# Final-state store no longer waited for at startup, one GLU block under the first norm, fourteen key copies on ScalarE

## What is computed

```python
q, k, v, u = project(x, w_in)                  # 1024 -> 4*512
a = diff_attention(q, k, v, ...)               # 4 heads
s, h_re, h_im = s5_mixer(u, ...)               # SSM scan; h_re, h_im: final states, outputs
#   inside: y = gelu(y); out = y * sigmoid(y @ w_glu + b_glu)        (the GLU)
x1 = layer_norm(ALPHA * x + concat(a, s) @ w_out, ln1_g, ln1_b)
# PEER: per token and each of 8 heads
q = rms_norm(x1 @ w_q); s = q . sub_keys; top 16 of each half, top 16 of 256 sums -> 128 experts in all
act = gelu(u_tab[idx] . x1);  out = sum(g * act * v_tab[idx])
y = layer_norm(ALPHA * x1 + out, ln2_g, ln2_b)
```

## Time and profile before

| what | value |
|---|---|
| three timed runs | 3626.15, 3635.01, 3638.67 us; median 3635.01 |
| profiled execution, time | 3620.71 us |
| its span, first to last instruction | 3618.9 us |
| busy share: PE, DVE, ACT, POOL | 71%, 67%, 42%, 35% |
| mean granted TensorE clock | 0.799 of full |
| DMA mean | 364 GB/s, 1316.28 MB |
| of it the expert gathers | 1140.92 MB in 1088 gathers |
| chain that ended last | DMA 29%, DVE 28%, PE 25%, ACT 7% |

### The profile page before, as it was taken

How to read it: one execution, slowest core, us unless ns; L and a number is a source line. 1 busy time by engine, 2 the same in 40 slices (tenths; PEclk the granted TensorE clock), 3 DMA queues, 4 the chain that set the end, 5 groups by cost and what they waited for, 6 DMA issues and landing times.

```text
span 3618.9 us, 44207 instructions
## 1 busy us (share of the span) xinstructions
PE 2575.2 (71%) x14060; PEld 1074.2 (30%) x14060; DVE 2420.2 (67%) x5555; ACT 1510.7 (42%) x4361; POOL 1272.2 (35%) x1099
## 2 busy tenths in 40 slices
PE   8967787866676667766775677677767766677666
PEld 5645443321133113312331233122312232332211
DVE  8626644686668656865596659765976587545874
ACT  2114344444544444444343444354435444454433
POOL 0001333334433443344434443444344434223244
PEclk9978898877787678767876787678867887988866
DMA  5257899999999999999999999999999999999988
GB/s 167 73 182 269 324 352 401 397 386 401 420 376 381 395 400 376 382 398 411 372 376 397 405 372 383 393 412 377 388 394 409 371 388 398 407 393 360 383 342 340
DMA packets 247448, 1316.28 MB, mean 364 GB/s; under 512 B 50498, under 2 KB 74850, under 8 KB 96802
## 3 DMA queue, kind: packets, MB, share of 16 engines
q0 software_dynamic: 156672, 1140.92, 78.3%
q1 hardware_dynamic: 78944, 160.54, 12.2%
q10 hardware_dynamic: 11602, 11.99, 1.0%
HBM read 1293.78 MB, written 17.97 MB: 362 GB/s over the span
## 4 chain that ended last, share of the span: by engine, by line
DMA 29%; DVE 28%; PE 25%; issue 8%; ACT 7%; POOL 1%; SPq 1%; DVEq 0%; POOLq 0%; ACTq 0%
DMA UV<-in_peer_uv,zone_x 26%; DVE zone_z L1661 12%; PE psum L1313 9%; PE psum L1234 3%; PE psum L379 3%; PE psum L519 3%; DMA wq<-in_cache_k 2%; PE psum L1254 2%; DVE zone_x L1560 2%; DVE zone_x L1563 2%; DVE zone_x L1561 2%; ACT D L1426 1%; DVE zone_x L1562 1%; POOL UV L1131 1%; ACT wge L1423 1%
## 5 line engine op out<-in xcount | busy, mean ns | idle before, releaser
L1313 PE MATMUL psum<-UV,D 64*64 64x512 f32 x8704 | 1505.3, 784 | 944.6 <-ACT D L1426 920.2
L1131 POOL DMA_INDIRECT UV<-in_peer_uv,zone_x x1088 | 1266.8, 1164 | 2248.7 <-PE psum L1313 1871.9
L1661 DVE CUSTOM_DVE_ANT_0 zone_z<-UV,zone_x 128x1024 bf16<-128x1024 f32 x1088 | 1333.6, 1226 | 775.0 <-DMA UV<-in_peer_uv,zone_x 705.1
L1421 ACT ACTIVATE ge<-acts 128x1 f32<-128x1 f32 x1088 | 219.7, 202 | 1650.7 <-DVE acts L1661 1646.6
L1313 PEld LDWEIGHTS psum<-UV,D 64*64 64x64 f32 x8704 | 311.3, 159 | 1823.7 <-issue 1792.4
L1426 ACT ACTIVATE D<-id,wge 128x64 f32<-128x64 f32 x1088 | 378.3, 348 | 35.4
L1423 ACT ACTIVATE wge<-ge,zone_x 128x1 f32<-128x1 f32 x1088 | 320.6, 295 | 35.5
L1254 PE MATMUL psum<-wq,zone_z 128*128 128x256 f32 (+1 forms) x1152 | 307.8, 427 | 1.2 <-ACT zone_z L1364 1.2
L1254 PEld LDWEIGHTS psum<-wq,zone_z 128*128 128x128 f32 (+1 forms) x1152 | 236.1, 210 | 117.2 <-issue 67.8
L1421 ACT ACT_TABLE_LOAD x115 | 147.5, 1283 | 2.8 <-ACT vrows L647 0.8
L1234 PE MATMUL psum<-w_out_sb,zone_z 128*128 128x512 f32 (+1 forms) x256 | 115.8, 606 | 0.0
(11 more groups left out here) (301 smaller groups left out, 2146.0 us busy)
## 6 DMA issues: line engine op xcount, KB each, us to landing
wq<-in_peer_w_q SPq DMA_DIRECT2D x72, 1024.0 KB, 9.2
UV<-in_peer_uv,zone_x POOLq DMA_INDIRECT x1088, 9.9
wq<-in_cache_k SPq DMA_DIRECT2D x64, 256.0 KB, 9.8
vrows<-in_cache_v SPq DMA_DIRECT2D x64, 256.0 KB
wq<-in_w_in SPq DMA_DIRECT2D x9, 1024.0 KB, 6.0
zone_x<-in_x_all SPq DMA_DIRECT2D x9, 512.0 KB, 8.3
UV<-in_w_out SPq DMA_DIRECT2D x2, 2048.0 KB, 14.3
w_out_sb<-in_w_out SPq DMA_DIRECT2D x1, 4096.0 KB, 33.1
```

The costliest lines, as they stand in the source:

```text
L1131: pool.indirect_dma_start(out=UV[:, n % RING, :], out_offset=None, in_=table, in_offset=bass.IndirectOffsetOnAxis(ap=icur[:, t % 2, column ...
L1313: ins = pe.matmul(bank[6 + r][q:q + 64, :], D[64 * r:64 * r + 64, n % RING, :], UV[64 * r:64 * r + 64, n % RING, DM + 512 * e:DM + 512 * e ...
L1421: act.activation(ge[:, j:j + 1], acts[:, j:j + 1], ACT.Gelu).then_inc(sem("gelu_done"), 1)
L1661: dve.tensor_tensor_reduce(out=junk[:, :], in0=UV[:, n % RING, 0:DM], in1=x1[:, t % 2, :], scale=1.0, scalar=0.0, op0=ALU.mult, op1=ALU.ad ...
```

## The change

Three edits:

1. DVE's wait for `h_out` at the end of `dve_startup` is gone. ACT waits for it ahead of L1373 of head 0, and DVE ahead of its first work at f = 25.
2. GLU block 1 moves on PE from place 20 to place 7 (right behind the output projection), into banks 6 and 7 instead of 1 and 3; its ACT part from 21 to 15, its DVE part from 23 to 19, its store from 24 to 20. Blocks 2 to 4 keep their places and banks.
3. The copies of transposed keys of units 0 to 13 move from DVE, one step after the next unit, to ACT, two steps after it and behind ACT's own copy of that unit.

```diff
-            return ((3, 5) if n < 4 else (1, 3))[n % 4 // 2]
+            return ((3, 5) if n < 4 else (6, 7) if n < 8 else (1, 3))[n % 4 // 2]
...
-            dve.wait_ge(sem("h_out"), 64)
...
-        def dve_unit_columns(dve, i):
+        def act_unit_columns(act, i):
...
-            dve.wait_ge(sem("k_T"), 4 + i + 1)
-            dve.tensor_copy(kT[:, 2 * blk:2 * blk + 2, t * P:t * P + r],
-                            bank[(1, 3)[i % 2]][:, 0:256].rearrange("p (h t) -> p h t", h=2)[:, :, :r])\
+            act.wait_ge(sem("k_T"), 4 + i + 1)
+            act.activation(kT[:, 2 * blk:2 * blk + 2, t * P:t * P + r],
+                           bank[(1, 3)[i % 2]][:, 0:256].rearrange("p (h t) -> p h t", h=2)[:, :, :r], ACT.Copy)\
                .then_inc(sem("k_Tcopied"), 1)
...
             if r == 1:
+                if n == 0:
+                    wait(act, "h_out", 64)
                 wait(act, "q_ps", n + 1)
...
-            if t == 0 and f - 1 in GLU_AT:
-                act_glu(act, 1 + GLU_AT.index(f - 1))
-            if t == 0 and f - 4 in GLU_AT:
-                act_glu_store(act, 1 + GLU_AT.index(f - 4))
+            if t == 0 and (f - 8 if f < base(0) + 20 else f - 1) in GLU_AT:
+                act_glu(act, 1 + GLU_AT.index(f - 8 if f < base(0) + 20 else f - 1))
+            if t == 0 and (f - 13 if f < base(0) + 25 else f - 4) in GLU_AT:
+                act_glu_store(act, 1 + GLU_AT.index(f - 13 if f < base(0) + 25 else f - 4))
...
                 wait(dve, "q_copied", EH * t + p1)
+                if t == 0 and g == 0:
+                    wait(dve, "h_out", 64)
...
-            if t == 0 and f - 3 in GLU_AT:
-                dve_glu(dve, 1 + GLU_AT.index(f - 3))
+            if t == 0 and (f - 12 if f < base(0) + 25 else f - 3) in GLU_AT:
+                dve_glu(dve, 1 + GLU_AT.index(f - 12 if f < base(0) + 25 else f - 3))
...
-        GLU_AT = [base(0) + 20, base(0) + 28, base(0) + 33, base(0) + 38]
+        GLU_AT = [base(0) + 7, base(0) + 28, base(0) + 33, base(0) + 38]
...
                             act_unit(act, i)
+                            if 1 <= i <= 14:
+                                act_unit_columns(act, i - 1)
...
-                        i = unit_at_step(t, k, 1)
-                        if i is not None and 1 <= i <= 14:
-                            dve_unit_columns(dve, i - 1)
```

## The result

The changed kernel runs in 3581.69 us (median of four, 3576.03 to 3587.49) against 3636.84 us for the kernel before in the same comparison: ratio 0.9853, 95% interval 0.9827 to 0.988, a gain of 44 to 63 us. The profiled execution took 3576.03 us with a span of 3574.2 us. The forecast was 3590 us, range 3572 to 3614.

What follows compares the result with a forecast made beforehand. Expert steps were taken as bound by what the gathers move, with room at startup and in the key units. 24.2 + 20.8 = 45 us off a 3635 median gives 3590 us, range 3572 to 3614.

Steps and rivals of the forecast that it cites:

- The moved waits: Startup: waits put in on ACT (near 252) and DVE (near 262) cost nothing while h_out lands at 231.5.
- The two halves of the sum: Startup, GLU block move: PE's clock stays up, 1.1 + 1.7 us; DVE's products leave head 0's last search, 3.6 us.
- 20.8: Key-unit stretch: 125.1 us, 40.0 MB, becomes 104.3 at the value units' 384 GB/s, a gain of 20.8 us.
- 95.6: Key-unit stretch: PE's time in us without its waits for D.
- The upper bound, 29.5: Key-unit stretch: the gain's other bound, PE's waits for D, 29.5 us in 20 places.
- The margin of 0.4 us on ACT: Key units: ACT's work after the transposes takes 2.1 us, PE's 2.5, so ACT arrives just in time.
- rival B: Key units: ACT takes over DVE's stall and hands it to D, so the copies win nothing; 3611 us, chance 0.18.
- 24.2: Startup: gain in us at the first gather, forecast at 269.2 instead of 293.45; bounds 20 and 30.
- rival C: DMA-bound part: gains given back as earlier gathers queue against other loads; 3630 us, chance 0.05.
- D: Key units: slower, ACT's in-order wait becomes PE's; 3649 us, chance 0.04.
- A: Startup or key units: larger gain, w_out no limit or the stretch follows PE's waits; 3576 to 3583 us, chance 0.18.

Runs made afterwards that it cites:

- edit1_only: The kernel before with only DVE's startup wait for the states' store removed and the two later waits put in; ratio 0.9971 (0.9951 to 0.999).
- edits1and2: The kernel before with the startup wait moved and GLU block 1 moved, key copies left on DVE; ratio 0.9943 (0.9927 to 0.996).
- edit3_only: The kernel before with only the key copies moved to ACT, startup as before; ratio 0.9919 (0.9894 to 0.9945).
- act_copy_early: The changed kernel with ACT making the key copies one step after the next unit, at DVE's old place; ratio 0.9864 (0.9811 to 0.9918).
- edit2_only: The kernel before with only GLU block 1 moved, DVE's startup wait in place; ratio 0.9998 (0.9977 to 1.002).
- glu_pe_part_only: The changed kernel with only GLU block 1's matmuls moved; its sigmoids, products and store back at places 21, 23 and 24; ratio 0.9858 (0.9824 to 0.9892).

## Why the prediction was right, and where it was off

**Edit 1.** L1234 was forecast to move by 17.9 us and moved by 251.53 - 233.51 = 18.0. Of its parts: start of the softmax 208.25 (208.14), start of L934 223.14 (223.05), its length 9.15 us against 9.3 (8.44 + 0.9). Two small errors cancel in the start of L934: the load was issued at 211.43 and not 211.05, and landed in 11.6 us and not 12.0. PE stood 5.25 us ahead of it and not 4.2, because the values (L926) took 1.16 us where the prediction left them their 2.07. The 0.5 MB store issued amid the load cost the load nothing that can be seen: it is the store that was held up (11.0 us to land in this trace, against 3.3 before). The moved waits cost nothing, as said. That the end moves by as much as the first gather did not show for this edit alone: 18.3 us became 10.3 in the profiled span.

**Edit 2.** Forecast 6.3; at the first gather it is 24.0 - 18.0 = 6.0 in the changed kernel, 6.7 alone, and 6.7 between edit1_only and edits1and2. The two halves of the sum stand too: 3.72 us for head 0's projection, and 3.7 us ahead of the last search that are gone (from the first search to it 7.9 us before, 4.3 after). The eight transposes took 1.09 us where the prediction put 0.9, for which it shows no row. ACT's table load took 1.28 us and its first sigmoid began 0.01 us behind it, so the sigmoids stayed under L1253, with 0.99 us to spare. The first gather was forecast at 269.2 and came at 269.41.

**Edit 3.** This is the term that was mis-sized: 20.8 us forecast, 28.6 in the trace (125.1 to 96.5), 29 in the timed ratio of edit3_only. The mechanism held: DVE's stall went, and with it PE's waiting for D, from 29.5 to 7.9 us, which is 21.6. The term that the sum left out is the other part of PE's time, which the prediction took as fixed (its "95.6"). The same 513 matmuls of the stretch were 95.63 us of busy PE before and 88.30 after, 7.3 us less; the 209 of L519 among them took 53.99 and 50.63. The mean granted clock was 0.92 before and 0.96 after. So it was in all fourteen profiles: 0.90 to 0.92 with 95.6 to 97.5 us of busy PE in the four that have DVE's early copies, 0.95 to 0.98 with 86.3 to 89.8 us in the ten others. Where PE stood less for D, its granted clock was higher.

The forecast came to 20.8 by another way, from the rate of the DMA, and that this is so near the 21.6 of the waits is luck. By its own terms the stretch moved 96.6 us x 396 GB/s = 38.3 MB where the forecast had 40.0 at 384 GB/s: 38.3 MB at 384 would be 99.6 us, so the bytes make 4.7 us and the rate 3. These two describe the shorter stretch and do not say what made it shorter. The upper bound, 29.5, was near the 28.6 by luck too: it takes all of PE's waits away and leaves its busy time, and neither was so. Nor is it shown that the DMA is now what limits the stretch. Its share is 1.00, but PE is busy or waiting for D in all but 0.4 of the 96.6 us, and a second profile of the same kernel has a shorter stretch with less busy PE, the same waits (8.3 us) and the same share:

```profile
356.60:451.20 94.60, 86.25 (x512) 49.75 (x508) 60.81 (x128) 45.56 (x136) 39.28 (x34) 0.98 1.00 398
```

The margin of 0.4 us on ACT that rival B doubted was enough. act_copy_early, where ACT does stand for the transposes with D behind them, lost 4 to 6 us and not 21.

**The sum.** 24.2 + 20.8 = 45 against a timed gain of 55 us (44 to 63). Tile 0 ended 51.6 us sooner in the profile, 7 more than the forecast's 45, as edit 3's 7.8 would have it; but the span shrank by 44.7 us. So the profiled execution, forecast at 3575.7 and measured at 3576.03, was met by luck: 7.8 us more in edit 3, and 7 fewer behind tile 0. The timed median, 3581.7, came 8 us under the forecast of 3590, which is the size of edit 3's surplus; but with 7 us of it missing in the profile and an interval of 44 to 63 us, the time doesn't show that this is the reason. These 7 us lie in the DMA-bound part: from the end of tile 0's steps to the last sum it took 2855.5 us in the profile before and 2862.3 after. Over all fourteen profiles this part lies between 2852 and 2866 us, with the five of the kernels that lack edit 3 or edits 1 and 2 (the kernel before among them) at 2852 to 2860 (median 2855.5) and the nine others at 2856 to 2866 (median 2860.1). Whether a part of the gain is really given back there, as rival C had it, or the executions merely differ, stays open; it is some 5 us between the medians and 7 of the 51.6 in this pair.

**The rivals.** B (ACT takes over the stall) and D (slower) did not happen. A was half right, on edit 3's side and not on that of `w_out`, and the measured 3581.7 lies in its span (3576 to 3583) as well as in the forecast's own (3579 to 3601), so the time does not part the two; the marks do. C stays open, as said.

## What to carry to other kernels

In a hand-ordered stream, a wait costs what is queued behind it on the way to the bound, so look first for the engine that runs ahead and is stopped: moving fourteen cheap copies one step later, on the same engine, was worth nearly as much as moving them to another (27.6 against 28.6 us). When a stall goes, look at the busy time of the engine that stood as well: here PE's own work in the stretch became 7.3 us shorter. When a wait is removed, read the landing times of the loads that the next instruction needs; the next limit is often already in the trace with its date. A gain of a few microseconds ahead of the first gather should be followed to a later mark before it is believed.

## What the runs showed of the hardware

Between the first gather and unit 1 every kernel here has the same instructions up to a shift. Eleven of the fourteen profiles need 87.7 to 88.7 us for it, three need 93.5 to 94.7 (edit2_only, edit3_only, glu_pe_part_only), and none lies between. Windows of 14 us from GLU block 4 on, first the kernel before, then edit2_only:

```profile
328.00:342.00 14.00, 11.17 (x74) 8.51 (x70) 7.99 (x30) 8.46 (x16) 2.81 (x3) 0.93 0.80 296
```

```profile
322.00:336.00 14.00, 14.00 (x69) 11.61 (x68) 5.40 (x22) 6.60 (x14) 0.97 (x2) 0.64 0.56 187
```

PE's rows there, again before and edit2_only:

```profile
326.36 1.79 PE L1313 MATMUL psum<-UV,D 64*64 64x512 f32 x8 [1.88 <-ACT D L1426]
328.08 1.22 PE L1266 MATMUL psum<-zone_y 128*128 128x128 f32 x4
329.09 4.13 PE L499 MATMUL psum<-kT,lng 128*128 128x64 f32 x32
333.06 3.67 PE L1254 MATMUL psum<-wq,zone_z 128*128 128x256 f32 x16
```

```profile
320.46 1.09 PE L1313 MATMUL psum<-UV,D 64*64 64x512 f32 x8 [1.88 <-ACT D L1426]
321.48 1.04 PE L1266 MATMUL psum<-zone_y 128*128 128x128 f32 x4
322.31 6.93 PE L499 MATMUL psum<-kT,lng 128*128 128x64 f32 x32
329.03 5.12 PE L1254 MATMUL psum<-wq,zone_z 128*128 128x256 f32 x16
```

The instructions are the same, both blocks begin 35.6 us behind the first gather, and the idle time ahead of them is the same 1.88 us; and yet the GLU block takes 4.13 us in one and 6.93 in the other, with a mean granted clock of 0.93 against 0.64 in the window: mostly 2.4 GHz, and mostly 1.2. In the kernel before, the matmuls just ahead of the block are the slow ones (L1313 1.79 us, against 1.09 in edit2_only) and the block is quick; in edit2_only these are quick and the block is slow, and so is the projection behind it (L1254, 5.12 us against 3.67). From the block's start to the projection's end that is 4.2 us, with no more behind it than the moment at which the clock was low; the rest of the 5.6 us between the two profiles comes later. The 5.6 us are nearly as much as the whole of edit 2, and they are why edit2_only has only 1.1 of its 6.7 us left at unit 1. The block takes 6.93 us in edit3_only and glu_pe_part_only too. Whether edit 2 alone brings this about or it was chance was not tried. Each run has one profile, so how often it comes is not known either; but edit3_only shows it without any change ahead of that place, and the changed kernel, with edit 2 in it, does not show it in any of its three profiles.
